# Routed experts in plain fp32 from raw weight blocks, gate and up in two 64-column tiles, with a ring of 21 blocks in place of 12 and the expert rows stored from ScalarE's queue

## What is computed

```python
g_p, g_idx = lax.top_k(g_prob, 1)                    # one of 4 groups
e_p, e_idx = lax.top_k(e_prob, TOP_K_IN_GROUP)       # two of its 8 experts
e_p = e_p / jnp.sum(e_p, axis=-1, keepdims=True)
...
hg = jax.nn.silu(jnp.einsum('nd,edf->nef', t, w_gate[sl])) * jnp.einsum('nd,edf->nef', t, w_up[sl])
out = out + jnp.einsum('nef,efd->nd', hg * combine[:, g, :, None], w_down[sl])
```

## Time and profile before

| | us |
|---|---|
| median of 3 runs | 996.49 (994.67 to 997.66) |
| the profiled execution | 994.84 |
| its span | 992.8 |
| busy in the span: PE, DVE, ACT, POOL | 826.4, 611.3, 514.1, 223.0 |

### The profile page before, as it was taken

The page is one execution under the profiler, slowest core; times in us unless marked ns, Lnnn a source line. Parts: engine busy times, 40 slices in busy tenths (PEclk is TensorE's granted clock), DMA queues, the critical chain, the costliest instruction groups (busy, mean ns, idle before and its releaser), DMA issues.

```text
span 992.8 us, 15658 instructions
## 1 busy us (share of the span) xinstructions
PE 826.4 (83%) x5633; PEld 696.5 (70%) x5633; DVE 611.3 (62%) x1054; ACT 514.1 (52%) x737; POOL 223.0 (22%) x278
## 2 busy tenths in 40 slices
PE   2999999778888798988787998938888888898980
PEld 2789999675555797977576898937666666666650
DVE  4482234454444346555365576467999999999963
ACT  5425444543333445353212243434898888888860
POOL 5000000001111001012322000002355555555522
PEclk9999999898999899999899999958999999999995
DMA  4332432236665343445555253647899999999715
GB/s 162 128 128 100 156 128 91 80 117 207 217 215 181 108 152 123 144 162 178 183 194 188 88 199 100 253 150 281 320 389 399 401 407 392 399 394 395 301 32 171
DMA packets 39697, 208.75 MB, mean 210 GB/s; under 512 B 5888, under 2 KB 6416, under 8 KB 20432
## 3 DMA queue, kind: packets, MB, share of 16 engines
q1 hardware_dynamic: 27760, 166.36, 45.7%
q0 software_dynamic: 11872, 41.54, 12.0%
HBM read 184.50 MB, written 23.38 MB: 209 GB/s over the span
## 4 chain that ended last, share of the span: by engine, by line
PE 39%; DVE 24%; ACT 16%; issue 10%; DMA 8%; POOL 1%; POOLq 1%; ACTq 0%; DVEq 0%; SPq 0%
PE bank L1669 14%; DVE rm L1555 9%; PE bank L1673 7%; ACT rm L979 4%; DMA fm<-in_state_C 4%; DVE rm L1074 3%; ACT rm L725 3%; PE bank L2008 2%; PE bank L2040 2%; ACT fm L1017 2%; PE bank L1659 2%; PE bank L1873 2%; DMA fm<-in_cache_lf 2%; DVE fm L1581 1%; PE bank L1824 1%
## 5 line engine op out<-in xcount | busy, mean ns | idle before, releaser
L1555 DVE TENSOR_TENSOR rm<-fm,rm 128x2048 fp32r<-128x2048 f32 x96 | 218.6, 2301 | 1.7 <-ACT rm L979 1.7
L1669 PE MATMUL bank<-rm 128*128 128x320 f32 x1344 | 210.0, 315 | 2.4 <-issue 1.6
L1669 PEld LDWEIGHTS bank<-rm 128*128 128x128 f32 x1344 | 201.3, 191 | 6.2 <-issue 4.5
L979 ACT ACTIVATE rm<-fm 128x2048 fp32r<-128x2048 f32 x96 | 182.7, 1906 | 0.4
L1074 DVE TENSOR_TENSOR rm<-fm,rm 128x2048 fp32r<-128x2048 f32 x48 | 110.0, 2293 | 103.5 <-ACT rm L725 103.3
L2008 PE MATMUL bank<-rm 128*128 128x256 f32 x1024 | 147.8, 293 | 29.2 <-POOL rm L656 14.2
L2008 PEld LDWEIGHTS bank<-rm 128*128 128x128 f32 x1024 | 129.1, 192 | 52.0 <-issue 28.8
L1673 PE MATMUL bank<-rm 128*128 128x256 f32 x960 | 128.9, 296 | 12.1 <-DVE rm L1074 7.3
L1673 PEld LDWEIGHTS bank<-rm 128*128 128x128 f32 x960 | 124.7, 204 | 14.1 <-DVE rm L1074 8.4
L725 ACT ACTIVATE rm<-fm 128x2048 fp32r<-128x2048 f32 x48 | 91.9, 1914 | 24.4 <-PE bank L1669 16.9
L2040 PE MATMUL bank<-rm 128*64 128x512 f32 x384 | 96.0, 399 | 2.5 <-issue 1.0
(11 more groups left out here) (373 smaller groups left out, 940.9 us busy)
## 6 DMA issues: line engine op xcount, KB each, us to landing
fm<-in_w_moe SPq DMA_DIRECT2D x96, 1024.0 KB, 8.1
fm<-in_w_dense SPq DMA_DIRECT2D x48, 1024.0 KB, 4.8
fm<-in_state_C SPq DMA_DIRECT2D x32, 257.0 KB, 5.4
out_C_sample<-fm POOLq DMA_DIRECT2D x32, 257.0 KB, 5.3
fm<-in_cache_kT POOLq DMA_DIRECT2D x16, 512.0 KB, 4.6
fm<-in_cache_v POOLq DMA_DIRECT2D x16, 512.0 KB, 4.6
y_rows<-fm POOLq DMA_DIRECT2D x32, 256.0 KB, 7.3
x_rows<-fm POOLq DMA_DIRECT2D x1, 1536.0 KB, 11.7
```

The costliest lines, as they stand in the source:

```text
L979: A_(e_half[m % NSPLIT][0], rawm[m % RAWM], ACT.Copy).then_inc(sem("e_hi"), 1)
L1555: TT(lo_half, rawm[m % RAWM], hi_half, ALU.subtract).then_inc(sem("e_split"), 1)
L1669: ins = mm(bank[b][:, 0:NT], w[:, k, P * u:P * (u + 1)], a[:, k, :], start=first, stop=final)
```

## The change

Weight blocks are no longer split. PE reads the raw blocks as plain fp32. Gate is computed into partitions 0 to 63 of a bank and up into partitions 64 to 127, by matmuls of 64 columns of weights (the tokens) that alternate between the two; down likewise puts its two halves of 512 columns in the two tiles. silu then reads 64 x 256 straight from the bank, DVE multiplies, PE turns, and one DVE copy brings the turned result to SBUF.

The area of `rm` is now also seen as fp32 (`em`); with it a ring of 21 block slots is formed (`slot`). The order of the blocks stays g0, u0, g1, u1, d0, g2, u2, d1 and so on. SP waits for the area that a slot lies in, later for `e_used` of the block that lay there, and from the fifth block on for the landing of the block four before it if that is an up or a down block (`FLIGHT`), which leaves four or five blocks under way.

The y of an expert is one ACT copy of 128 x 512 into one of three buffers, and ACT itself issues its store. POOL only packs tokens. The page table is loaded by SP among the small tensors at the start. The loops over experts are written out.

```diff
         rawm = [take(UN) for _ in range(RAWM)]
...
+        halves = {q: em[:, q:q + UN] for q in (0, UN, 2 * UN, 3 * UN, 8192, 8192 + UN, 13312, 13312 + UN, 13312 + 2 * UN)}
+        slot = [halves[8192], halves[8192 + UN], rawm[2], rawm[3], rawm[4], rawm[0], rawm[1],
+                halves[13312], halves[13312 + UN], halves[13312 + 2 * UN]] + rawm[5:12] + \
+               [halves[q * UN] for q in range(4)]
...
@@ SP
+            small_in(pt, A["page_table"])
...
-            with sp.Fori(1, NE // EB - 1) as i:
-                for q in range(RAWM):
-
-                    sp.wait_ge(sem("e_split"), i * RAWM - RAWM + q + 1)
-                    load(lambda blk: i * EB + blk, q)
...
+                elif n >= NSLOT:
+
+                    sp.wait_ge(sem("e_used"), n - NSLOT + 1 if n < 3 * NE - 1 else unit(NE - 8, 2) + 1)
+                if n >= FLIGHT and order[n - FLIGHT][1] > 0:
+                    sp.wait_ge(*landed(*order[n - FLIGHT]))
+                load(n)
...
@@ ACT
-                A_(e_half[m % NSPLIT][0], rawm[m % RAWM], ACT.Copy).then_inc(sem("e_hi"), 1)
...
+                A_(yrow[v % NY], bank[4 + v % 2][:, :], ACT.Copy).then_inc(sem("e_y_taken"), 1)
+                act.wait_ge(sem("e_y_taken"), v + 1)
+                act.dma_start(halves_of(y_rows[v * CAP:(v + 1) * CAP, :]), yrow[v % NY])\
+                    .then_inc(sem(f"e_y_stored{v % NY}"), 16)
...
+                A_(act_g[v % 2][CAP:2 * CAP, :], bank[v % 2][0:CAP, 0:FE], ACT.Silu).then_inc(sem("e_silu"), 1)
...
@@ DVE
-                TT(lo_half, rawm[m % RAWM], hi_half, ALU.subtract).then_inc(sem("e_split"), 1)
...
+                TT(hact[e % 2][0:CAP, :], bank[e % 2][CAP:2 * CAP, 0:FE], act_g[e % 2][CAP:2 * CAP, :], ALU.mult)\
+                    .then_inc(sem("e_hact"), 1)
+                dve.wait_ge(sem("e_hT_full"), e + 1)
+                CP(htp[e % 2], cube(bank[2 + e % 2][:, 0:2 * CAP], 2)).then_inc(sem("e_hT"), 1)
...
@@ PE
+                for k in range(KC):
+                    last_g = mm(bank[b][0:CAP, 0:FE], x[:, k, :], g[:, k, :], start=(k == 0), stop=(k == KC - 1),
+                                skip_group_check=True)
+                    last_u = mm(bank[b][CAP:2 * CAP, 0:FE], x[:, k, :], u[:, k, :], start=(k == 0), stop=(k == KC - 1),
+                                skip_group_check=True)
+                    if k == 3 and between:
+                        between()
...
+                for k in range(2):
+                    for j in range(2):
+                        ins = mm(bank[b][CAP * j:CAP * (j + 1), :], hT[:, k, :], w[:, k, 512 * j:512 * (j + 1)],
+                                 start=(k == 0), stop=(k == 1), skip_group_check=True)
```

More of the change, by code:

```diff
@@ L359, in hybrid_step, with unit, weights, landed @@
         mxi = [im[:, 56 + 24 * i:56 + 24 * (i + 1)].bitcast(U32) for i in range(2)]
[L361 to L381, removed]
+        def unit(v, j):
+            if j == 2:
+                return 3 * v + 4 if v < NE - 1 else 3 * v + 2
+            return j if v == 0 else 3 * v - 1 + j
+        order = {unit(v, j): (v, j) for v in range(NE) for j in range(3)}
+        def weights(v, j):
+            n = unit(v, j)
+            return slot[n % NSLOT]
+        def landed(v, j):
+            name = f"e_down_in{v % 7}" if j == 2 else f"e_gate_up_in{v % 8}"
+            return sem(name), 16 * (v // 7 + 1) if j == 2 else 32 * (v // 8 + 1)
+        crowd_w = [rawm[0], rawm[1], rawm[2]]
+        c_in, c_in0 = landed(NE - 1, 2)
         def either(eng, crowd, calm):
@@ L392, in either, with halves_of @@
             eng.nop()
+        def halves_of(rows):
+            return rows.rearrange("s (h c) -> h s c", h=2)
         block = ctx.enter_context(nc.Block())
@@ L439, in load @@
[L439 to L447, removed]
-            for q in range(RAWM):
-                if q < RAW1:
-                    sp.wait_ge(sem("split_done"), NCH - RAW1 + 1 + q)
-                elif q == RAW1:
+                    sp.dma_start(xr[:, 0:2, :], A["x_prompt"]).then_inc(sem("rows_in"), 16)
@@ new lines, in start, with turn_h @@
+            def start(v, between=None):
+                pe.wait_ge(sem("e_packed"), v + 1)
+                if v >= 2:
+                    pe.wait_ge(sem("e_hact"), v - 1)
+                pe.wait_ge(*landed(v, 0))
+                last_g, last_u = gate_up(v % 2, pack[v % 2], weights(v, 0), weights(v, 1), between)
+                last_g.then_inc(sem("e_used"), 1)
+                last_u.then_inc(sem("e_used"), 1)
+            start(0)
+            for v in range(NE):
+                def turn_h():
+                    pe.wait_ge(sem("e_hact"), v + 1)
+                    transposes(2 + v % 2, hact[v % 2]).then_inc(sem("e_hT_full"), 1)
+                if v + 1 < NE:
+                    start(v + 1, turn_h)
+                else:
+                    turn_h()
+                pe.wait_ge(*landed(v, 2))
+                pe.wait_ge(sem("e_hT"), v + 1)
+                if v >= 2:
+                    pe.wait_ge(sem("e_y_taken"), v - 1)
+                down(4 + v % 2, htp[v % 2], weights(v, 2)).then_inc(sem("e_used"), 1)
@@ new lines, in crowd @@
+            def crowd():
+                with pe.Fori(0, NE) as e:
+                    for j in range(JB):
+                        n = e * JB + j
+                        pe.wait_ge(c_in, n * 48 + c_in0 + 48)
+                        pe.wait_ge(sem("e_packed"), n + NE + 1)
+                        gate_up(0, pack[0], crowd_w[0], crowd_w[1])[1].then_inc(sem("e_used"), 1)
+                        pe.wait_ge(sem("e_hact"), n + NE + 1)
+                        for i in range(2):
+                            ins = mm(bank[2][:, CAP * i:CAP * (i + 1)], hact[0][0:CAP, P * i:P * (i + 1)],
+                                     ident[0:CAP, 0:CAP], start=True, stop=True)
+                        ins.then_inc(sem("e_hT_full"), 1)
+                        pe.wait_ge(sem("e_hT"), n + NE + 1)
+                        down(4, htp[0], crowd_w[2]).then_inc(sem("e_used"), 1)
```

305 lines of the change are left out of this document (108 added, 197 removed).

## The result

The changed kernel takes 1078.18 us (1075.93 to 1079.32), the kernel before 997.08 us beside it. The ratio is 1.0815 (95% interval 1.0788 to 1.0842): 8.2% slower, where 940 us, 5.6% faster, was forecast. The profiled execution has a span of 1075.9 us, against 992.8.

A forecast was written before the change was run, and what follows sets the result against it. DVE's split bounds the experts, transfers close behind. Sort end 685.3, plus 2.1 fixed, 197.5 for 79 blocks, 22.5 for y, 4.6 to the last copy's end, 24.7 to span end, 2.04 around it, 1.65 to the median: 940 us, range 932 to 956.

The forecast's parts named there:

- the y term of "the transfers": Expert stage: storing one expert's y, 0.262 MB in 2 KB pieces, takes 0.75 us; 22.5 us for 30 stores.
- signs of being wrong: DMA share well below 1.00 after 700, loads waiting for PE (`e_used`), or the sort ending later than 686.
- The rival for "slower": Experts on PE: two tiles not side by side, at half clock, 10.9 us an expert, 1067 us in all; chance 0.03.
- the price of PE: PE per expert: gate and up 1.97 us, down 1.0, transposes 0.3; 3.3 us, or 6.6 at half clock, under the transfers.
- my sentence that the rows don't agree: Plain fp32 on PE: 0.22 us a matmul of 256 columns, two passes at 2.4 GHz, against the skill's four.
- The split left and transfers are next: Expert stage: without the split DMA is the bound, 8.25 us an expert against 8.6, 11 us in all.
- a last store at 912.0 + 2.9: Stage end: sort ends at 685.3, last block lands at 907.4, y copy ends at 912.0, then a store of 2.89.
- The blocks ahead of the sort: Weight prefetch: 17 blocks landed when the sort ends, 79 to come at 2.50 us each.
- the cap: Blocks under way: four move 419 GB/s, 2.50 us a block; a rival had the cap throttle, 3.05 us, 961; chance 0.07.
- The tail: After the last y copy: store, gather and sums, 24.7 us to the end of the span, the same as before.
- The rival "the rate stays at 397": Transfers after the sort: 397 GB/s is all a stream mixed with stores gives, 228.5 us for 220.0, 949; chance 0.18.
- the rate falls: Transfers after the sort: the rate falls under a continuous stream, by a tenth of 397, 253 us, 973; chance 0.03.

The follow-up runs named there:

- the kernel with plain stores: The changed kernel with each half of y stored separately as 64 rows from ACT's queue, in place of one store of outermost size 2: 937.03 us.
- the kernel with the low cap: The kernel with two plain y stores from ACT's queue, with FLIGHT lowered from 4 to 1: 1059.34 us.
- the four kernels with plain stores: Changed kernel with y stored as two plain halves: from ACT 937.03 us, from POOL 937.67, with a size-4 form that folded to 64 939.35, with FLIGHT 9 938.24.

## Why the prediction was wrong

**The step that failed** is the y term of "the transfers": "0.63 by bytes, and double, 1.25; I take 0.75". Both bounds assumed that 16 engines share the store, because those of the rows did. It measured 5.1 us on the two engines that carry it, and an expert 12.0 us in place of 8.25. I priced bytes and the size of a piece, and didn't look at how the pieces are dealt out, though the new line has "halves" as its outermost size and another queue issues it. The store before had its 64 rows outermost and went from POOL's queue; form and queue changed together. The runs tell them apart: a plain store costs the same from either queue (937.03 and 937.67), and with outermost size 2 a store has two engines from either, but 1078 us from ACT's and 980 from POOL's. The term was put at 22.5 us for 30 stores; by the sum it is 32 x 5.13 = 164, and the whole stage took 139.8 us more than with plain stores.

Of the signs of being wrong that I had named, the first is what showed: a DMA share of 0.71 after 720. The sort ended later than 686 too (687.61), but in the runs here it ends anywhere from 682.6 to 693.6, so this sign tells nothing.

**The rival for "slower" came near the time by chance.** It gave 1063 to 1067, for two tiles that don't run side by side. They do. In the kernel with plain stores:

```profile
760.57 0.38 PE L1933 MATMUL bank<-fm,em 128*64 128x256 f32 x1
760.57 0.38 PE L1935 MATMUL bank<-fm,em 128*64 128x256 f32 x1
760.78 0.38 PE L1933 MATMUL bank<-fm,em 128*64 128x256 f32 x1
760.79 0.38 PE L1935 MATMUL bank<-fm,em 128*64 128x256 f32 x1
```

Two lines of the source, less than 10 ns apart, a new pair every 0.21 us. I had given it 0.03, and had no rival for the store, so nothing in the forecast led to the measured time for the right reason.

**A second step was wrong and, by luck, did no harm: the price of PE.** I put an expert at 3.3 us. It takes 5.6, as the rows of 961 to 988 show, at a granted clock of 1.00. The source has 8 turns of L1932 an expert, and the trace has 16 records of it (512 for 32 experts): one matmul in plain fp32 stands in the trace as two records. The `x2` in the earlier trace rows is thus one matmul of 256 columns, not two, and the `x16` of 1.97 us is eight. A plain fp32 matmul of 256 columns takes 2 x 0.215 = 0.43 us, 256 x 4 / 2.4 GHz. So the four passes that the Trainium skill gives for true FP32 ("FP8 and Floating Point Precision", TensorE Precision Notes) are what the trace shows, and my sentence that the rows don't agree was a misreading. At the level of 1.2 GHz a pair takes twice as long. In the kernel with the low cap, where PE had waited 5.48 us for a block and the granted clock was 0.50:

```profile
833.82 0.63 PE L1933 MATMUL bank<-fm,em 128*64 128x256 f32 x1
833.85 0.63 PE L1935 MATMUL bank<-fm,em 128*64 128x256 f32 x1
834.25 0.64 PE L1933 MATMUL bank<-fm,em 128*64 128x256 f32 x1
834.28 0.63 PE L1935 MATMUL bank<-fm,em 128*64 128x256 f32 x1
```

There it is 0.43 a pair, and an expert would be 2 x 5.6 = 11.2 us by estimate, above the 8.1 of the transfers. I had written that PE is under the transfers "either way", and that it would be busy less than half of the stage. With plain stores it is busy for 84% of it at a granted clock of 0.95. The forecast of this part held because PE kept its clock, for which I gave no reason.

**What held.** The split left and transfers are next: 422 GB/s in one even stage once the store is spread. The stage was forecast from 685.3 to a last store at 912.0 + 2.9, 229.6 us; the four kernels with plain stores have 226.5 to 226.9. The blocks ahead of the sort are worth 12 us, the cap nothing. The tail is unmoved: 1053.95 to 1075.9 is 22.0 us, and 971.37 to 992.8 was 21.4. The rival "the rate stays at 397" falls, as does "the rate falls": 422. Forecast 940, and 937 with the store mended.

**The version that beats both** is the one with two plain stores: 937.03 us, 6.0% under the kernel before and 13% under the changed one.

## What to carry to other kernels

Price a transfer by the engine that has most of it to carry: look at the outermost size that is left after folding, on both sides, and at the queue that issues it, before bytes and pieces. A transfer whose form or queue changes is a new transfer, and its price in the old trace doesn't go with it. In a trace, a DMA share that stands at a few sixteenths while only stores are under way (0.13 here), and stores that take many times their bytes, give this away at once. So do completions short of 16 a store from ACT's queue; from POOL's there were 16 even where two engines carried the store.

## What was not expected of the hardware

- A store with outermost size 2 is carried by two engines from ACT's queue (130 packets, share 0.13 alone) and from POOL's too (share 0.13 alone), but there with 448 packets of 8 B beside its 64 pieces (528 packets), and without leaving the other engines idle (399 GB/s in place of 281).
- Two overloaded engines slow every other transfer: weight blocks and y together went from 422 to 281 GB/s with y 8% of the bytes.
- Issuing a transfer can hold the engine that issues it: up to 19 us on ACT in the changed kernel, with at most three stores under way. What sets this limit no run here shows.
- A matmul in plain fp32 is two records in the trace; 256 columns take 0.43 us at the full clock, and a second tile of 64 columns runs beside it at no cost.
- A block of 1 MB takes 5.1 us with one or two under way, twice its 2.5 us of transfer; the rate is then 265 GB/s, and with five or ten under way 421 to 422.
